# Sixty-one products of a zero operand on the matrix engine, in five places where it waits

## The reference, cut to what matters

```
for layer in (0, 1):
    hn = rms_norm(h, mix_norm[layer])
    mix = hybrid_mixer(hn, ...)   if layer == 0        # linear attention + stick-breaking attention
          conformer_conv(hn, ...) if layer == 1        # gated projection, conv of 31 taps, layer norm, projection
    h = h + mix
    h = h + swiglu(rms_norm(h, ffn_norm[layer]), wg, wu, wd)
# second block
p, pc = modulate(x, ...) @ w_in, modulate(ctx, ...) @ w_in
y = concat([attention, gated_scan, fourier_mix]) @ w_out
x = x + g1 * y
x = x + g2 * swiglu_ffn(modulate(x, ...), w_gate_up, w_down)
return rms_norm_2(x, final_norm_g)
```

## Time and profile before

| | us |
|---|---|
| median of 3 runs | 1113.61 |
| lowest, highest | 1112.51, 1115.98 |
| the profiled execution's own time | 1115.49 |
| its span, first to last instruction | 1113.7 |
| outside the span (launch and end) | 1.8 |
| PE busy | 1051.3 (94%) |
| DVE busy, ACT busy | 644.4 (58%), 506.8 (46%) |
| mean granted clock of PE | 0.974 |

### The profile page before, as it was taken

One profiled execution on the slowest core, in us unless ns is written; L12 is line 12 of the kernel. 1 busy time (PEld: TensorE's weight loads), 2 busy tenths in 40 slices (PEclk: granted clock), 3 DMA queues, 4 the chain that ended last, 5 costly groups with the idle time before them and its releaser, 6 DMA issues.

```text
span 1113.7 us, 16603 instructions
## 1 busy us (share of the span) xinstructions
PE 1051.3 (94%) x7158; PEld 909.9 (82%) x7158; DVE 644.4 (58%) x709; ACT 506.8 (46%) x575; POOL 68.5 (6%) x84
## 2 busy tenths in 40 slices
PE   7998999999999997999999998999898879999997
PEld 6996888888888784988888887898557768888886
DVE  5656548666676552657776554353558654444544
ACT  6467454444445233644444443454456444444332
POOL 0001200000000000000010000000226000000000
PEclk9999999999999998899999999999989889999999
DMA  6541447666762774347788554222000335555451
GB/s 259 194 172 51 179 159 251 230 239 226 245 213 84 238 230 142 121 181 269 265 298 288 182 180 179 109 93 97 1 1 2 115 116 187 189 188 176 170 183 39
DMA packets 34046, 187.69 MB, mean 169 GB/s; under 512 B 3776, under 2 KB 8128, under 8 KB 15296
## 3 DMA queue, kind: packets, MB, share of 16 engines
q1 hardware_dynamic: 25920, 155.66, 39.5%
q0 software_dynamic: 7200, 27.27, 7.2%
q10 hardware_dynamic: 864, 3.88, 0.9%
HBM read 181.09 MB, written 1.05 MB: 164 GB/s over the span
## 4 chain that ended last, share of the span: by engine, by line
PE 86%; DVE 5%; ACT 4%; DMA 2%; issue 1%; SPq 1%; POOL 0%; DVEq 0%; ACTq 0%
PE PS L269 12%; PE PS L271 12%; PE PS L270 12%; PE PS L534 11%; PE PS L535 11%; PE PS L536 11%; PE PS L997 2%; DMA raw<-wstream 1%; PE PS L434 1%; PE PS L547 1%; PE PS L298 1%; PE PS L299 1%; PE PS L300 1%; DMA U<-CU 1%; ACT w_hi L252 1%
## 5 line engine op out<-in xcount | busy, mean ns | idle before, releaser
L256 DVE TENSOR_TENSOR w_lo<-raw,w_hi 128x2048 fp32r<-128x2048 f32 x140 | 320.6, 2292 | 223.3 <-ACT w_hi L252 223.3
L252 ACT ACTIVATE w_hi<-raw 128x2048 fp32r<-128x2048 f32 x141 | 269.1, 1911 | 209.4 <-PE PS L271 103.2
L534 PE MATMUL PS<-w_hi,a_hi 128*128 128x512 f32 x528 | 211.7, 401 | 4.4 <-DVE a_lo L460 4.2
L535 PE MATMUL PS<-w_lo,a_hi 128*128 128x512 f32 x528 | 208.2, 394 | 0.0
L536 PE MATMUL PS<-w_hi,a_lo 128*128 128x512 f32 x528 | 208.2, 394 | 0.0
L269 PE MATMUL PS<-a_hi,w_hi 128*128 128x256 f32 (+1 forms) x608 | 187.5, 308 | 15.5 <-DVE a_lo L1897 5.0
L271 PE MATMUL PS<-a_hi,w_lo 128*128 128x256 f32 (+1 forms) x608 | 182.9, 301 | 0.0
L270 PE MATMUL PS<-a_lo,w_hi 128*128 128x256 f32 (+1 forms) x608 | 182.8, 301 | 0.0
L269 PE MATMUL PS<-h_hi,w_hi 128*128 128x256 f32 x528 | 149.9, 284 | 0.4 <-DVE h_lo L699 0.4
L271 PE MATMUL PS<-h_hi,w_lo 128*128 128x256 f32 x528 | 149.4, 283 | 0.0
L270 PE MATMUL PS<-h_lo,w_hi 128*128 128x256 f32 x528 | 149.4, 283 | 0.0
(11 more groups left out here) (304 smaller groups left out, 1085.9 us busy)
## 6 DMA issues: line engine op xcount, KB each, us to landing
raw<-wstream SPq DMA_DIRECT2D x142, 1024.0 KB, 4.9
modraw<-wmod POOLq DMA_DIRECT2D x48, 512.0 KB, 5.0
U<-CU SPq DMA_DIRECT2D x32, 142.0 KB, 4.5
cst<-cst ACTq DMA_DIRECT2D x1, 1632.0 KB, 9.9
mlw<-mlw ACTq DMA_DIRECT2D x1, 1280.0 KB, 5.8
X<-xT SPq DMA_DIRECT2D x2, 512.0 KB, 5.3
CROW<-crow POOLq DMA_DIRECT2D x1, 1024.0 KB, 5.2
CTX<-ctxT POOLq DMA_DIRECT2D x1, 1024.0 KB, 8.5
```

The source lines that it names most:

```text
L252: nc.scalar.activation(w_hi[:, slot, :], raw[:, rslot, :], ACT.Copy).then_inc(S("hi_done"), 1)
L256: dve.tensor_tensor(w_lo[:, slot, :], raw[:, rslot, :], w_hi[:, slot, :].bitcast(F32), ALU.subtract).then_inc(S("lo_done"), 1)
L534: nc.tensor.matmul(out, a_hi[:, k, src, ts], wh, start=k == 0, stop=False, skip_group_check=True)
L535: nc.tensor.matmul(out, a_hi[:, k, src, ts], wl, start=False, stop=False, skip_group_check=True)
```

## The change

A helper on PE issues n products of `zero` with itself, 128x512, into a bank of PSUM. It is called in five places, 61 products in all. No wait, no semaphore and no other instruction is added, taken away or moved.

```diff
+        def idle_products(bank, n):
+
+            for _ in range(n):
+                nc.tensor.matmul(PS[:, bank, :], zero[:, 0:P], zero, start=True, stop=True)
...
             sb_z(0)
             sb_z(1)
             qk_ss(3)
+            idle_products(7, 10)
             sb_between(0)
...
             i.then_inc(S("ln_sum"), 1)
+            idle_products(0, 10)
             for k in range(KT):
                 pe.wait_ge(S("ln_sq"), k // 4 + 1)
                 i = nc.tensor.matmul(PS[:, 6, T:2 * T], ones, SQ[:, k, :], start=k == 0, stop=k == KT - 1)
             i.then_inc(S("ln_ss"), 1)
+            idle_products(0, 16)
             out_units_pe(pe, U_PW2, "cv", 2, 1)
             ffn_pe(pe, 1, "ffn1", 3, 4)
+            idle_products(7, 12)
 
             pe.wait_ge(S("x_updated"), 16)
...
             out_units_pe(pe, U_OUT2, "o2", 4, sums=5)
+            idle_products(7, 13)
             ffn_pe(pe, 2, "ffn2", sums=6)
```

## The result

22 runs of each kernel, in turn, gave 1115.02 us before (1109.75 to 1120.36) and **1108.55 us** after (1104.25 to 1113.56): a ratio of 0.9942, with an interval of 0.9927 to 0.9956. That is 6.5 us less. The forecast was 1107.5 us, faster, in a range of 1104.0 to 1112.0; it held.

The account below looks back on a forecast made before the run. PE bounds the kernel, with 86% of the chain. 1.6 + 2.8 + 0 + 1.4 + 2.5 = 8.3 us off the profiled 1115.5 gives 1107.2; 5.65 off the median gives 1108.0. Forecast 1107.5 us, range 1104.0 to 1112.0.

Parts of the forecast that it names:

- The products cost nothing: All five waits: products 0.22 us apart end before the awaited work, leaving rests of 0.8 to 1.5 us.
- Place 1: Attention, PE's 3.02 us wait for DVE's `SBM`: ACT starts on the scores at 102.5, gaining 1.6 us (0 to 1.6).
- the stretch at 110.61: Half-speed stretch after PE's 1.72 us rest for POOL; might go too, another 1.5 us at best, not counted.
- Place 2: 3.22 us wait for ACT's squares: the sum's 16 records take 3.7 us instead of 6.49, gaining 2.8 us.
- Place 3: 4.99 us wait before the second projection, whose pairs come at DVE's pace: -1.7 to +0.3 us, taken as 0.
- The low stretch that I feared between the pairs: Second projection: PE rests 0.7 us between DVE's pairs and may fall to half speed again, costing at most 1.7 us.
- Place 4: 3.60 us wait for DVE's `a_lo`: the projection's 19th product starts at 680.4 instead of 681.86, gaining 1.4 us.
- Place 5: 4.24 us wait: 13 products take 3.0 us instead of 5.54, gaining 2.5 us that reaches the end whole.
- The step from the profile to the median: Profiled execution, 1.9 us above the median, has longer low stretches; against the median the gain is 5.65 us, not 8.3.
- the first rival: All five waits: the clock falls in spite of the products of zero, gain 0, 1113.6 us; chance 0.15.
- The second: Rival: clock held, but 1.7 us lost between pairs and 1.6 us in the stick-breaking chain; 1110.5 us, chance 0.18.
- The third: Rival: PE enters waits at half speed and products outlast them, 6.0 us over all five; 1119.6 us, chance 0.04.

Follow-up runs that it names:

- e8: Changed kernel with twice as many full-size products (20, 20, 32, 24, 26): 1111.67 us, ratio to before 0.9972.
- e2: Changed kernel with only the 10 products of place 1, the other calls taken out: 1112.34 us, ratio to before 0.9988.
- e6: Changed kernel without the 16 products of place 3, 6 runs: 1105.96 us, ratio to before 0.9918.
- e9: Changed kernel without place 3's products, with products in three more waits (14, 10, 6): 1101.74 us, ratio to before 0.9881.
- e11: The changed kernel measured again, 12 runs: 1108.51 us, ratio to before 0.9942.
- e12: Changed kernel with half as many products (5, 5, 8, 6, 6): 1110.55 us, ratio to before 0.9957.
- e5: The changed kernel measured again, 6 runs: 1107.98 us, ratio to before 0.9938.
- e10: Changed kernel without the 16 products of place 3, measured again with 10 runs: 1107.03 us, ratio to before 0.9932.

## Why the prediction was right, point by point

**The products cost nothing.** They were 0.21 to 0.22 us apart, ended 0.9 to 1.5 us ahead of what PE waited for (forecast 0.8 to 1.5), the awaited product came neither earlier nor later for them, and e8 gives the price when they outlast the wait: 0.8 to 1.0 us per place, except at place 3.

**Place 1, 1.6 us.** ACT at 102.60 (forecast 102.5), the first output product 7.51 us behind the awaited one instead of 9.12, so 1.6 us sooner, the last `sb_out` product 2.0 to 2.3 us sooner; the part above 1.6 comes with the stretch at 110.61, which was not counted. The doubt that `sb_z(3)` waits for DVE was right, it does, for 1.62 us, and it does not matter. The low stretch at 110.61 stayed away in e2, e6, e8, e9, e11 and e12 as well as in the first profile; in e5 and e10 one stands at 105, behind the new rest of 1.62 us.

**Place 2, 2.8 us.** 3.72 us for the 16 records against 3.7, in every profile with ten products. The gain of 2.8 holds against the profile of before and is, on average over four profiles without the products, nearer 1.5.

**Place 3, 0.** Right, and for the reason given: the pairs come every 1.46 us and PE's clock hardly matters there. PE's rests between them were 0.1, 0.5 and 0.5 us and not 0.7. The low stretch that I feared between the pairs did not appear in the three profiles of the change.

**Place 4, 1.4 us.** The 19th product started 4.6 us behind the first (forecast 4.3, before 5.8); the stage is shorter by 1.2.

**Place 5, 2.5 us.** The 14th product started 3.2 us behind the first (forecast 3.0, before 5.54), and the stage is shorter by 2.4. The product rows of the kernel after:

```profile
906.11 2.75 PE L276 MATMUL PS<-zero 128*128 128x512 bf16 x12
910.30 0.47 PE L539 MATMUL PS<-w_hi,a_hi 128*128 128x512 f32 x1 [1.44 <-DVE a_lo L465]
...
913.51 0.39 PE L540 MATMUL PS<-w_lo,a_hi 128*128 128x512 f32 x1
```

**The step from the profile to the median** was the weak one. I read the profiled execution of before as unlucky, 1.9 us above the median of three runs, and took 2.65 us off the gain for it. With 22 runs that median is 1115.02: the profiled execution stands 0.5 us above it, and the three runs were on the low side. So the ground that I gave for taking something off, that the profiled execution was unlucky as a whole, does not stand. The thing itself is half true. At place 2 the stretch was of the long kind in the profile of before and shorter or absent in three others, which takes 1.3 us off on average. At place 5 it was 6.8 us long in all four profiles without products, so that nothing was to be taken off there. With 2.2, 1.5, 0, 1.2 and 2.3 us the places make 7.2 us (an estimate from the table), and the medians are 6.5 us apart, with an interval of 1.6 us either way. The forecast took 6.1 us, from a median that was 1.4 us low: that it came out within 1.1 us owes something to luck, as it was the middle between two sums of which one took too much off.

**The rivals.** Zeros are seen: the low stretches are gone at all five places, so the first rival is out. What the Trainium skill, "TensorE: Matmul & The Clock Gate", section "Seeing it yourself", says of another limiter, on the current, that all-zero operands don't trip it, does not carry over to this gate by these runs; of that other limiter no run here shows anything. The second, a gain that does not travel, is out for place 1. The third did not come up: PE entered all five waits at full speed.

**What I had not priced** is the rest of the program. Each execution has low stretches at other places, and they move: 17 to 27 us of them in the profiles of the same changed kernel, with 8.5 us lost in the convolution's stage in one and nothing in the others. The range was wide enough for that, but nothing in the sum said so.

## What to carry to other kernels

Look at the granted clock behind each long wait of PE. If it is at half speed and what stands there is PE's own work, fill the wait with full-size products into a free bank, so many that a rest of 1 to 1.5 us is left; where PE then works at the pace of another engine, as at place 3, it brings nothing. A stretch in one profile of before is not there in every execution: see in several how long it is before its price goes into the sum. Take the sum of such a change from the stages of several profiles and the effect from many runs: here the same program differs by 10 us from run to run, more than the whole gain.

## What the runs showed of the hardware

An engine that is busy in all its records can still lose its clock. 56 records of one-column products took 9.77 us without a gap and ran at 0.50 for most of that, while products of zeros with 512 columns in the same waits kept it at 1.00. In these runs products of zeros held the clock, and a PE that the profile shows as busy throughout did not.

The length of a rest does not settle whether the clock falls. One of 2.1 us in the output projection was followed by half speed in all 13 profiles that have it, one of 1.62 us at place 1 in 2 of 8, while one of 3.21 us (e2, place 2) and one of 2.94 us (e12, place 5) were not.

The low stretches ahead of the program's end measured 3.40, 6.81 or 10.2 us or near these in all profiles, and differ between executions of one program in number and place; in the 22 runs the mean clock lay between 0.983 and 0.990 for the changed kernel, and the spans between 1102.4 and 1111.6 us. For one microsecond less at half speed the medians gave 0.28 us (6.5 us for some 23). Much of the spread is this too: over the 27 runs of the kernel before that stand beside e11, the time rises by 0.36 us for each microsecond at half speed, with a correlation of 0.96. At half speed PE's own work takes twice as long, so that a low stretch takes half its length from it at most, and hardly anything where another engine sets the pace (place 3: 46.8 us in e6 with a stretch of 6.8 us, 46.5 in e5 and e11 without one at that place).
